# State space outputs of a fused two-block layer written feature by token instead of token by feature

## Chip, cores and metric

One core of a Trainium2 chip runs the whole program in one launch. The metric is the device time of that launch in microseconds (us), the median of three runs before the change.

## What is computed

Two transformer-like blocks on 512 tokens of width 1024, in fp32. The first has latent attention, chunked attention and a mixture of experts. The second has dilated attention and, beside it, a state space part with 16 heads of 64 features, 2 groups, state width 128 and chunks of 128 tokens; only this part and what surrounds it is touched. Cut to what matters:

```python
decay = jnp.exp(segsum(adt))                                   # per head, 128 x 128, lower triangle
cb = jnp.einsum('bclgn,bcsgn->bcgls', cc, bc)
y_diag = jnp.einsum('bcgjls,bcsgjp->bclgjp', cb[:, :, :, None] * decay, xg)   # inside a chunk
states = jnp.einsum('bcsgn,bcsgjp->bcgjpn', bc, xg * decay_to_end)
prev = ...                                                     # h = h * chunk_decay + state, chunk by chunk
y_off = jnp.einsum('bclgn,bcgjpn->bclgjp', cc, prev) * state_decay            # from the chunks before
y = y_diag + y_off + d_skip * xs_h                             # skip term
y_ssm = rms_norm_2(y * silu(z_ssm), ssm_norm_g)                # the gate z is a projection of the block's input
```

Then `y_att` and `y_ssm` go through one output projection (2048 to 1024), a residual and a layer norm.

## The kernel before, in words

Each engine has its own hand-written instruction list (`block.tensor`, `block.vector` for DVE, `block.scalar` for ACT, `block.gpsimd` for POOL, `block.sync` for SP's loads), tied together by counting semaphores. Within an engine, the order of the code is the order of execution. Activations lie feature by token (features on partitions, 512 tokens along the free axis) in eight tiles RA to RH of 128 x 8 x 512; the state space part works token by feature within a chunk.

**Gate tiles.** The 16 column tiles of the gate projection z (`gate_tile`, L1165, matmuls L689 to L691) are 24 matmuls of 128 x 512 each. Weights arrive in a ring of eight slots; ACT rounds each to fp32r (`hi`, L1411) and DVE takes the remainder (`lo`, L1788), so a gate tile needs both. Ten of the tiles are spread among the steps of the state space part, six follow. ACT evicts each with SiLU (`gate_out`, L1689); POOL multiplies it into the attention output RB (tiles 0 to 7) or the state space output (8 to 15) in `product` (L2661); ACT squares the product (`gated`, L1395) and DVE adds the squares (`sq_add`, L1793) for the norm. `stats_summed` (L745, L747) sums them over partitions; `root` (L1402, L1403) makes the factor.

**The state space part.** RG holds the convolved inputs feature by token, RH the same turned to token by feature (L1176). For each chunk c of four:

- PE spreads the cumulative sums over partitions (`spread_sums`, L1207, banks 2 and 3), DVE takes differences (L2382, 8 operations of 128 columns per half chunk), ACT the exponential (L1681), POOL the product with C times B (`decays`, L2643). The result is `decay`, a 128 x 128 matrix per head, in RE.
- POOL computes skip vector times x into RG (`skip_and_scale`, L2629), then scales x by dt in place in RH (L2633).
- PE multiplies, head by head, with `decay` stationary and the head's 64 columns of x moving: 16 matmuls into banks 4 and 5, token by feature (L1236). DVE adds the two banks onto RG (L2407).
- From chunk 1 on, PE multiplies C with the state (L1246, banks 0 and 1), DVE scales the result into `y_off` (L2415), scales the state (L2421) and adds `y_off` onto RG (L2422).
- POOL scales x for the states (`keys`, L2653), PE computes them into banks 4 and 5 (L1253), DVE sums them into the state (L2432, L2434).

PE's order for chunk c is: heads, first half of the next chunk's spreading, state output, gate tile 3 + 2c, states, second half of the spreading, gate tile 4 + 2c. After the fourth chunk and gate tile 9, PE turns the whole output back to feature by token: 32 turns of 128 x 128 in eight banks (L1264). DVE and ACT evict four banks each into RH (L1782, L1380). Then come the statistics of the attention half and gate tiles 10 to 15. The output projection (`parts`, L1271) takes each half as two fp32r parts: attention in RG and RE, state space in RF and RH.

Of the kernel before, what the change touches and what calls it, by code (L numbers as in the profile page):

```python
# [19 lines left out]
F32 = mybir.dt.float32  # L20
# [6 lines left out]
P = 128  # L27
# [49 lines left out]
def build(nc, xT_d, vec_d, rows_d, pos_d, rel_d, wr_d, wdt_d, pre_d, moe_d, post_d, out_d):  # L77
    ctx = ExitStack()
    with ctx:
# [139 lines left out]
        xg_tok, y_tokT = (r.rearrange("p (t h c) -> p t h c", t=TT, h=SSM_H) for r in (RHf, RGf))  # L219
# [135 lines left out]
        skip_ok = sem("skip_ok")  # L355
# [144 lines left out]
        PE_YT = PE_ZA + Z_BEHIND - 1  # L500
        PE_ZB = PE_YT + 8
        PE_OUT = PE_ZB + 16 - Z_BEHIND
        assert all(e % 2 == 0 for e in (PE_U, PE_OT, PE_O, PE_H, PE_Q2, PE_OT2, PE_XBC, PE_Z0, PE_YT, PE_ZB))

        def bank(e):
            if PE_XT <= e < PE_BT:
                return ps[e - PE_XT]
            if PE_YT <= e < PE_ZB:
                return ps[YT_BANKS[e - PE_YT]]
            return ps[(e - PE_Q2) % 4] if PE_Q2 <= e < PE_OT2 else ps[6 + e % 2]  # L510
# [24 lines left out]
        YT_BANKS = (0, 1, 4, 5, 6, 7, 0, 1)  # L535
# [119 lines left out]
        def _(pe):  # L655
# [3 lines left out]
            def free_bank(e):  # L659
# [8 lines left out]
                elif PE_YT <= e < PE_ZB:  # L668
                    pe.wait_ge(ev[e % 2], PE_YT // 2 + (e >= PE_YT + 6))
# [559 lines left out]
            for c in range(TT):  # L1229
                if c > 0:  # L1230
                    pe.wait_ge(state_ok, c)
                pe.wait_ge(xg_ok, c + 1)
                for h in range(SSM_H):
                    if h % 4 == 0:
                        pe.wait_ge(mm_ok, 4 * c + h // 4 + 1)
                    last = mm(ps[4 + h // 8][:, (h % 8) * 64:(h % 8) * 64 + 64], decay[:, h, :], xg_tok[:, c, h, :],  # L1236
                              start=True, stop=True)
                last.then_inc(yd_full, 1)

                if c < TT - 1:  # L1240
                    spread_sums(c + 1, (0, 1))
                if c > 0:
                    pe.wait_ge(cb_ok, 2)
                    pe.wait_ge(y_tok, c)
                    for g in range(2):
                        last = mm(ps[g][:, :], RF[:, 2 + g, c * P:(c + 1) * P], state[:, g, :], start=True, stop=True)  # L1246
                    last.then_inc(yo_full, 1)
                gate_tile(3 + 2 * c)
                if c < TT - 1:
                    pe.wait_ge(xgd_ok, c + 1)  # L1250
                    pe.wait_ge(yd_ok, c + 1)
                    for g in range(2):
                        last = mm(ps[4 + g][:, :], b_tok[:, g, c, :], REf[:, 2048 + g * T:2048 + (g + 1) * T], start=True, stop=True)  # L1253
                    last.then_inc(st_full, 1)
                    spread_sums(c + 1, (2, 3))
                    gate_tile(4 + 2 * c)

            pe.wait_ge(y_tok, TT)
            for i in range(8):
                e = PE_YT + i  # L1260
                t, hf = i // 2, i % 2
                free_bank(e)
                for c in range(4):
                    last = nc.tensor.transpose(bank(e)[:, c * P:(c + 1) * P],  # L1264
                                               RGf[:, t * D + (hf * 4 + c) * P:t * D + (hf * 4 + c + 1) * P], ident[:, :])
                last.then_inc(acc, 1)
# [4 lines left out]
            parts = (two(RGr, REr), two(RFr, RHr))  # L1271
# [94 lines left out]
        def _(act):  # L1366
# [324 lines left out]
            def gated(i):  # L1691
# [4 lines left out]
                else:  # L1696
                    k = i - KT
                    square(ST_SS, k, RH[:, k, :])
                    A(RFr[:, k, :], RH[:, k, :], ACT.Copy, scale=V("ssm_g", k)).then_inc(s_hi, 1)
# [28 lines left out]
            for i in range(1, 8, 2):  # L1728
                e = PE_YT + i
                evict(e, ([(RH[:, 4:8, (i // 2) * P:(i // 2 + 1) * P], quad(bank(e)[:, :]))], 1.0))  # L1730
# [7 lines left out]
            for i in range(Z_BEHIND, 16):  # L1738
# [5 lines left out]
                if i < Z_BEHIND + 4:  # L1744
                    j = 2 * (i - Z_BEHIND)
                    mix_parts(RGr, RB, (j, j + 1))
# [21 lines left out]
        def _(dve):  # L1768
# [631 lines left out]
            lo(M_Z + 4)  # L2400
            dve.wait_ge(sp2, 3)
# [363 lines left out]
```

## Time and profile before

| | |
|---|---|
| median of 3 runs | 1289.07 us (1288.01 to 1290.4) |
| the profiled execution, its own time | 1283.11 us |
| its span, first to last instruction | 1281.3 us |
| PE busy | 1201.3 us (94%) |
| DVE busy | 633.3 us (49%) |
| ACT busy | 464.3 us (36%) |
| POOL busy | 170.0 us (13%) |
| mean granted clock of TensorE | 0.979 |

Busy time is the union of an engine's instructions over the whole span; it says little about a stage of 75 us in it. The profiled execution is one run, and lies a little under the median of the three others. In the rows further down, PE is the matmul engine, PEld its weight loads; an fp32 matmul appears as two records (passes), and a record such as `128*64 128x128` names the part of the array used (rows * columns) and the moving operand.

### The profile page before, as it was taken

To read this page: it belongs to the slowest core of one execution; us is meant where nothing else is said; L and a number is where in the kernel's file an instruction comes from. 1 tells how busy PE (TensorE), PEld (TensorE's weight loads), DVE (VectorE), ACT (ScalarE), POOL (GpSimd) and SP (SyncE) were. 2 spreads that over 40 slices of the span, in tenths; PEclk is the share of its full clock that TensorE was granted. 3 is DMA by queue.
4 is the path that set the end of the run, shared out by engine and by line. 5 is a ranking of instruction groups with operands and counts; after the bars stand their busy time and mean duration, and the time that the engine had idled before them with its cause. 6 is when DMAs were issued, how large, how long until landed. Compare 5 with 4: busy or idle time off the path is not lost.

```text
span 1281.3 us, 17052 instructions
## 1 busy us (share of the span) xinstructions
PE 1201.3 (94%) x6666; PEld 863.8 (67%) x6666; DVE 633.3 (49%) x1167; ACT 464.3 (36%) x839; POOL 170.0 (13%) x145
## 2 busy tenths in 40 slices
PE   3899899999999999999999799999999999998995
PEld 0567676778887664455444378897558788777883
DVE  1755467654444454312101465334667666857546
ACT  3324346642222321111111351124665365655314
POOL 1300020000000000000000201600600038612003
PEclk8899999999999999999989899999999999999998
DMA  9565261023337559999999813321002221212301
GB/s 359 217 217 197 97 247 67 2 80 92 96 96 295 193 216 402 412 412 412 411 411 411 328 60 94 93 94 66 2 1 68 97 67 50 66 58 76 97 17 66
DMA packets 59166, 215.91 MB, mean 169 GB/s; under 512 B 4736, under 2 KB 5128, under 8 KB 59088
## 3 DMA queue, kind: packets, MB, share of 16 engines
q1 hardware_dynamic: 53040, 195.71, 41.8%
q10 hardware_dynamic: 3600, 10.21, 2.0%
q0 software_dynamic: 2448, 8.91, 1.9%
q8 instruction: 54, 0.88, 0.3%
q14 instruction: 24, 0.20, 0.0%
HBM read 200.37 MB, written 14.44 MB: 168 GB/s over the span
## 4 chain that ended last, share of the span: by engine, by line
PE 83%; DMA 5%; DVE 4%; issue 4%; ACT 4%; POOL 1%; SPq 0%; ACTq 0%; DVEq 0%; POOLq 0%
PE ps L689 13%; PE ps L691 12%; PE ps L690 12%; PE ps L993 7%; PE ps L975 5%; PE ps L1048 4%; PE ps L817 3%; PE ps L794 3%; PE ps L804 2%; DMA ring<-in_w_pre 2%; PE ps L730 2%; PE ps L732 2%; PE ps L731 2%; PE ps L759 2%; DMA ring<-in_w_moe 2%
## 5 line engine op out<-in xcount | busy, mean ns | idle before, releaser
L1788 DVE TENSOR_TENSOR ring_r<-ring,ring_r 128x1024 fp32r<-128x1024 f32 x115 | 143.6, 1251 | 185.4 <-ACT ring_r L1411 184.7
L1411 ACT ACTIVATE ring_r<-ring 128x1024 fp32r<-128x1024 f32 x116 | 121.4, 1053 | 206.1 <-PE ps L691 166.5
L689 PE MATMUL ps<-RB_r,ring_r 128*128 128x512 f32 x320 | 126.3, 395 | 1.1 <-DVE RH L1832 1.1
L691 PE MATMUL ps<-RB_r,ring_r 128*128 128x512 f32 x320 | 124.6, 389 | 0.0
L689 PE MATMUL ps<-RC_r,ring_r 128*128 128x512 f32 x224 | 90.1, 402 | 1.5 <-DVE ring_r L1788 1.2
L691 PE MATMUL ps<-RC_r,ring_r 128*128 128x512 f32 x224 | 87.3, 390 | 0.0
L690 PE MATMUL ps<-RD_r,ring_r 128*128 128x512 f32 x224 | 87.3, 390 | 0.0
L690 PE MATMUL ps<-RG_r,ring_r 128*128 128x512 f32 x208 | 81.0, 390 | 0.0
L689 PEld LDWEIGHTS ps<-RB_r,ring_r 128*128 128x128 f32 x320 | 60.1, 188 | 16.8 <-issue 4.5
L691 PEld LDWEIGHTS ps<-RB_r,ring_r 128*128 128x128 f32 x320 | 60.1, 188 | 12.6
L2608 POOL DMA_INDIRECT RC<-expert_rows,small x4 | 3.9, 963 | 457.7 <-DMA expert_rows<-RD 456.8
L2087 DVE TENSOR_SCALAR RH<-ps,small 128x256 f32<-128x256 f32 x64 | 28.0, 479 | 72.3 <-PE ps L975 72.1
L975 PE MATMUL ps<-RD_r,RC_r 128*128 128x256 f32 x256 | 61.3, 297 | 1.2 <-DVE RD_r L2067 1.2
L993 PE MATMUL ps<-ring,RH 128*64 128x512 f32 x272 | 61.3, 595 | 0.0
L2174 DVE TENSOR_TENSOR MASK<-RB,ps 128x256 f32<-128x256 f32 (+1 forms) x17 | 7.2, 421 | 105.3 <-ACT RB L1546 99.3
L975 PE MATMUL ps<-RD_r,RG_r 128*128 128x256 f32 x256 | 58.3, 283 | 0.0
L975 PEld LDWEIGHTS ps<-RD_r,RC_r 128*128 128x128 f32 x256 | 48.2, 200 | 12.6 <-issue 12.6
L1546 ACT ACTIVATE RB<-ps 128x256 f32<-128x256 f32 (+1 forms) x17 | 6.5, 384 | 133.2 <-PE ps L993 115.6
L730 PE MATMUL ps<-ring_r,RB_r 128*128 128x256 f32 x192 | 54.5, 284 | 0.2 <-DVE RF L1782 0.2
L732 PE MATMUL ps<-ring_r,RB_r 128*128 128x256 f32 x192 | 54.3, 283 | 0.0
L1424 ACT ACTIVATE SB<-ps,small 128x512 f32<-128x512 f32 (+1 forms) x64 | 40.2, 631 | 33.3 <-issue 17.3
L689 PEld LDWEIGHTS ps<-RC_r,ring_r 128*128 128x128 f32 x224 | 42.0, 188 | 13.4 <-issue 2.2
(496 smaller groups left out, 2652.2 us busy)
## 6 DMA issues: line engine op xcount, KB each, us to landing
ring<-in_w_moe SPq DMA_DIRECT2D x48, 1024.0 KB, 16.0
ring<-in_w_post SPq DMA_DIRECT2D x68, 512.0 KB, 3.6
ring<-in_w_pre SPq DMA_DIRECT2D x48, 512.0 KB, 3.7
ring<-in_w_pre SPq DMA_DIRECT2D x16, 1024.0 KB, 6.9
RE<-in_w_moe SPq DMA_DIRECT2D x16, 1024.0 KB, 14.1
RF<-in_w_moe SPq DMA_DIRECT2D x16, 1024.0 KB, 14.7
PQ<-in_w_moe SPq DMA_DIRECT2D x8, 1024.0 KB, 16.4
RB<-in_w_moe SPq DMA_DIRECT2D x8, 1024.0 KB, 16.7
```

Source lines behind the costliest of these rows:

```text
L689: mm(out, part(m)[:, w], xh(k), start=first and k == 0, stop=False)
L690: mm(out, part(m)[:, w], xl(k), start=False, stop=False)
L691: ins = mm(out, remainder(m)[:, w], xh(k), start=False, stop=last and k == n_k - 1)
L730: mm(out, xh(k)[:, tok], hi_w, start=(k == 0), stop=False)
L732: last = mm(out, xh(k)[:, tok], lo_w, start=False, stop=(k == KT - 1))
L794: mm(ps[2 * (n % 2) + s][:, 0:w], ql(2 * p + s, t), kr(2 * p + s, w), start=True, stop=True).then_inc(s_full, 1)
L975: last = mm(ps[GATHER_BANKS[i]][:, k % 2 * 256:k % 2 * 256 + 256], (h2_hi, h2_lo)[s][:, t, k * P:(k + 1) * P], OHr[:, quad % 2, t, :], sta ...
L993: last = mm(ps[2 + p % 2][u * SLOTS:(u + 1) * SLOTS, :], Xg[:, buf, kk, c:c + SLOTS], moe_tile(at + s, u, k), start=(kk == 0), stop=(kk == ...
L1048: last = mm(ps[4 + hf][u * SLOTS:(u + 1) * SLOTS, :], hidT[:, p % 2, f, u * SLOTS:(u + 1) * SLOTS], moe_tile(at + f, u, hf), start=(f == 0 ...
L1411: A(part(m), tile, ACT.Copy).then_inc(w_hi, 1)
L1424: A(probs(n)[:, s, 0:w], ps[2 * (n % 2) + s][:, 0:w], ACT.Exp, scale=-1.0, bias=nmax(n, s), accum_out=sums(n, s)).then_inc(p_ready, 1)
L1788: v.tensor_tensor(remainder(m), arrival(m)[2], part(m).bitcast(F32), ALU.subtract).then_inc(w_split, 1)
```

## The change

The output of the intra-chunk step is written feature by token at once.

- **Heads.** x (64 columns of a head) becomes the stationary operand and `decay` the moving one. The result is 64 features by 128 tokens; even heads go to partitions 0 to 63, odd ones to 64 to 127 of the same columns. Eight pairs fill banks 4 and 5.
- **State part.** For chunks 1 to 3, the scaled `y_off` is turned by PE (8 turns of 128 x 128) into banks 4 and 5 first, opening the accumulation to which the heads then add.
- **Skip term.** The product on POOL is gone. DVE evicts each 128 x 128 block with one operation, RG = RG * d + bank, with d as a column per feature (`d_col`, two small copies). RG keeps x feature by token until then and holds the output afterwards.
- **States** go to banks 0 and 1, directly behind the heads; POOL's `keys` moves ahead of the last two decay products. The differences for the first half of the next chunk now follow the state sum on DVE, and those of the second half open the next chunk.
- **Order on PE** for chunk c: state output, gate tile 2 + 2c, turns (these from chunk 1 on), heads, states, first half of the spreading, gate tile 3 + 2c, second half (these up to chunk 2). Then gate tile 9, statistics, gate tiles 10 to 15.
- The 32 final turns and their eight evictions are gone. RG and RH change places behind it (products, squares, the fp32r parts).

The diff, cut to its core:

```diff
@@ tensor @@
             for c in range(TT):
                 if c > 0:
                     pe.wait_ge(state_ok, c)
+                    for g in range(2):
+                        last = mm(ps[g][:, :], RF[:, 2 + g, c * P:(c + 1) * P], state[:, g, :], start=True, stop=True)
+                    last.then_inc(yo_full, 1)
+                    gate_tile(2 + 2 * c)
+                    pe.wait_ge(yd_ok, c)
+                    pe.wait_ge(y_tok, c)
+                    for k in range(KT):
+                        mm(ps[4 + k // 4][:, k % 4 * P:k % 4 * P + P], y_off[:, 2 * k:2 * k + 2, :], ident[:, :],
+                           start=(k % 4 == 0), stop=False, is_transpose=True)
                 pe.wait_ge(xg_ok, c + 1)
                 for h in range(SSM_H):
                     if h % 4 == 0:
                         pe.wait_ge(mm_ok, 4 * c + h // 4 + 1)
-                    last = mm(ps[4 + h // 8][:, (h % 8) * 64:(h % 8) * 64 + 64], decay[:, h, :], xg_tok[:, c, h, :],
-                              start=True, stop=True)
+                    out = ps[4 + h // 8][64 * (h % 2):64 * (h % 2) + 64, h // 2 % 4 * P:h // 2 % 4 * P + P]
+                    last = mm(out, xg_tok[:, c, h, :], decay[:, h, :], start=(c == 0), stop=(c == 0 or h % 8 >= 6))
                 last.then_inc(yd_full, 1)
 
                 if c < TT - 1:
+                    if c == 0:
+                        pe.wait_ge(cb_ok, 2)
+                    pe.wait_ge(xgd_ok, c + 1)
+                    for g in range(2):
+                        last = mm(ps[g][:, :], b_tok[:, g, c, :], REf[:, 2048 + g * T:2048 + (g + 1) * T], start=True, stop=True)
+                    last.then_inc(st_full, 1)
                     spread_sums(c + 1, (0, 1))
-                if c > 0:
-                    pe.wait_ge(cb_ok, 2)
-                    pe.wait_ge(y_tok, c)
-                    for g in range(2):
-                        last = mm(ps[g][:, :], RF[:, 2 + g, c * P:(c + 1) * P], state[:, g, :], start=True, stop=True)
-                    last.then_inc(yo_full, 1)
-                gate_tile(3 + 2 * c)
-                if c < TT - 1:
-                    pe.wait_ge(xgd_ok, c + 1)
-                    pe.wait_ge(yd_ok, c + 1)
-                    for g in range(2):
-                        last = mm(ps[4 + g][:, :], b_tok[:, g, c, :], REf[:, 2048 + g * T:2048 + (g + 1) * T], start=True, stop=True)
-                    last.then_inc(st_full, 1)
+                    gate_tile(3 + 2 * c)
                     spread_sums(c + 1, (2, 3))
-                    gate_tile(4 + 2 * c)
-
-            pe.wait_ge(y_tok, TT)
-            for i in range(8):
-                e = PE_YT + i
-                t, hf = i // 2, i % 2
-                free_bank(e)
-                for c in range(4):
-                    last = nc.tensor.transpose(bank(e)[:, c * P:(c + 1) * P],
-                                               RGf[:, t * D + (hf * 4 + c) * P:t * D + (hf * 4 + c + 1) * P], ident[:, :])
-                last.then_inc(acc, 1)
+
+            gate_tile(9)
             stats_summed(ST_AT, KT, 2)
@@ vector @@
+            for s in range(2):
+                ins = v.tensor_copy(d_col[64 * s:64 * s + 64, :], rows[64 * s:64 * s + 64, R_DSKIP + s:R_DSKIP + 16:2])
+            link(ins)
             dve.wait_ge(sp2, 3)
             for c in range(TT):
-                dve.wait_ge(skip_ok, c + 1)
-                dve.wait_ge(yd_full, c + 1)
-                for g in range(2):
-                    yt = y_tokT[:, c, 8 * g:8 * g + 8, :]
-                    ins = v.tensor_tensor(yt, yt, h8(ps[4 + g][:, :]), ALU.add)
-                link(ins)
-                dve.sem_inc(yd_ok, 1)
-                if c < TT - 1:
-                    differences(c + 1, (0, 1))
                 if c > 0:
+                    differences(c, (2, 3))
                     dve.wait_ge(yo_full, c)
...
-                    link(v.tensor_tensor(y_tokT[:, c, :, :], y_tokT[:, c, :, :], y_off, ALU.add))
-                dve.sem_inc(y_tok, 1)
-                sq_add_mixed(2 * c)
-                lo(M_Z + 5 + 2 * c)
+                    sq_add_mixed(2 * c - 1)
+                    lo(M_Z + 4 + 2 * c)
+                dve.wait_ge(yd_full, c + 1)
+                for k in range(KT):
+                    y = RG[:, k, c * P:(c + 1) * P]
+                    ins = v.scalar_tensor_tensor(y, y, d_col[:, k:k + 1], ps[4 + k // 4][:, k % 4 * P:k % 4 * P + P],
+                                                 ALU.mult, ALU.add)
+                ins.then_inc(yd_ok, 1)
                 if c < TT - 1:
-                    differences(c + 1, (2, 3))
                     dve.wait_ge(st_full, c + 1)
...
+                    differences(c + 1, (0, 1))
+                sq_add_mixed(2 * c)
+                lo(M_Z + 5 + 2 * c)
@@ gpsimd @@
                 decays(c, (0, 1))
                 product(2 * c)
-                if c == 0:
-                    keys(0)
+                if c < TT - 1:
+                    keys(c)
                 decays(c, (2, 3))
-                if 0 < c < TT - 1:
-                    keys(c)
                 product(2 * c + 1)
                 if c + 1 < TT:
-                    skip_and_scale(c + 1)
-            pool.wait_ge(ev[0], PE_ZB // 2)
-            pool.wait_ge(ev[1], PE_ZB // 2)
+                    scaled(c + 1)
+            pool.wait_ge(yd_ok, TT)
```

## Rows read from the trace of the kernel before

**Rows 1.** The page's chain that ended last, share of the span by engine.

```profile
PE 83%; DMA 5%; DVE 4%; issue 4%; ACT 4%; POOL 1%; SPq 0%; ACTq 0%; DVEq 0%; POOLq 0%
```

**Rows 2.** Windows, chunk 1: PE busy (x), PEld, DVE, ACT, POOL, PEclk, DMA.

```profile
1077.10:1097.60 20.50, 20.50 (x121) 16.03 (x120) 18.27 (x30) 12.02 (x14) 14.98 (x10) 1.00 0.18 52
```

**Rows 3.** Timeline of PE in chunk 1: start us, us, engine, line, tiles.

```profile
1077.14 3.68 PE L1236 MATMUL ps<-RH,RE 128*128 128x64 f32 x32
1080.74 1.16 PE L1207 MATMUL ps<-w_r,ident 64*128 64x128 f32 x16
1081.84 1.98 PE L1246 MATMUL ps<-RF 128*128 128x512 f32 x4
1083.26 0.79 PE L689 MATMUL ps<-RC_r,ring_r 128*128 128x512 f32 x1
...
1089.14 1.88 PE L1253 MATMUL ps<-RE,RF 128*128 128x512 f32 x4
1090.95 1.16 PE L1207 MATMUL ps<-w_r,ident 64*128 64x128 f32 x16
```

**Rows 4.** Timeline of PE, the last turns and the statistics.

```profile
1128.88 0.60 PE L1264 MATMUL ps<-ident,RG 128*128 128x128 f32 x4
1129.79 3.28 PE L1264 MATMUL ps<-ident,RG 128*128 128x128 f32 x28 [0.31 <-ACT SB L1689]
1132.90 1.02 PE L745 MATMUL ps<-PQ,ones 128*128 128x512 f32 x2
```

**Rows 5.** Timeline of PE in the attention, where two heads use the column halves.

```profile
901.71 0.66 PE L804 MATMUL ps<-ident,PQ 128*128 128x128 f32 x4
902.30 0.88 PE L817 MATMUL ps<-PTB,RE 128*64 128x128 f32 x12
903.11 0.49 PE L794 MATMUL ps<-RD,RC 64*128 64x128 f32 x4
...
907.35 1.09 PE L817 MATMUL ps<-PTB,RE 128*64 128x128 f32 x16
908.37 0.70 PE L794 MATMUL ps<-RD,RC 64*128 64x256 f32 x4
```

**Rows 6.** Timeline of DVE in chunk 1.

```profile
1080.93 1.29 DVE L2407 TENSOR_TENSOR RG<-RG,ps 128x512 f32<-128x512 f32 x2 [1.44 <-PE ps L1236]
...
1085.75 3.46 DVE L2421 TENSOR_TENSOR RF<-RF,MASK 128x512 f32<-128x512 f32 x2
1089.14 1.21 DVE L2422 TENSOR_TENSOR RG<-RG,RE 128x1024 f32<-128x1024 f32 x1
...
1092.24 2.15 DVE L2382 TENSOR_SCALAR RE<-ps,MASK 128x128 f32<-128x128 f32 x8
1094.31 1.28 DVE L2434 TENSOR_TENSOR RF<-RF,ps 128x512 f32<-128x512 f32 x2
```

**Rows 7.** Lines by form on DVE: count | busy us, mean ns.

```profile
L2460 DVE SCALAR_TENSOR_TENSOR RB<-RB,vec,RINV 128x512 f32<-128x512 f32 x8 | 8.7, 1130 | 0.0
...
L2247 DVE SCALAR_TENSOR_TENSOR RA<-ps,small,RA 128x512 f32<-128x512 f32 x8 | 6.0, 751 | 10.6 <-PE ps L1125 10.6
```

**Rows 8.** Timeline of POOL at the end of chunk 1.

```profile
1094.10 2.56 POOL L2643 TENSOR_TENSOR RE<-RE,OTK 128x512 f32<-128x512 f32 x2 [5.44 <-ACT RE L1681]
1096.61 2.90 POOL L2653 TENSOR_TENSOR RE<-RH,MASK 128x1024 f32<-128x1024 f32 x1
1099.47 1.72 POOL L2661 TENSOR_TENSOR RB<-RB,SB 128x512 f32<-128x512 f32 x1
```

**Rows 9.** Timeline of ACT after gate tiles 9 and 10.

```profile
1129.14 0.60 ACT L1689 ACTIVATE SB<-ps 128x512 f32<-128x512 f32 x1 [7.45 <-PE ps L691]
1129.63 0.62 ACT L1395 ACTIVATE PQ<-RB 128x512 f32<-128x512 f32 x1
...
1140.35 1.28 ACT L1689 ACT_TABLE_LOAD   x1 [1.75 <-PE ps L691]
```

**Rows 10.** Windows, as in rows 2, of the slice with the clock at half.

```profile
1172.00:1176.00 4.00, 4.00 (x12) 3.16 (x11) 3.55 (x5) 2.68 (x4) 0.60 (x2) 0.57 0.04 11
```

More of the change, by code:

```diff
@@ L217, in build @@
         chosen = OTK[:, 0, 0:TT * N_EXP].rearrange("p (t e) -> p t e", t=TT)
-        xg_tok, y_tokT = (r.rearrange("p (t h c) -> p t h c", t=TT, h=SSM_H) for r in (RHf, RGf))
+        xg_tok = RHf.rearrange("p (t h c) -> p t h c", t=TT, h=SSM_H)
+        d_col = small[:, 240:248]
         decay = REf[:, 0:2048].rearrange("p (h l) -> p h l", h=SSM_H)
@@ L499, in build @@
         PE_ZA = PE_BT + 2
-        PE_YT = PE_ZA + Z_BEHIND - 1
-        PE_ZB = PE_YT + 8
+        PE_ZB = PE_ZA + Z_BEHIND - 1
         PE_OUT = PE_ZB + 16 - Z_BEHIND
-        assert all(e % 2 == 0 for e in (PE_U, PE_OT, PE_O, PE_H, PE_Q2, PE_OT2, PE_XBC, PE_Z0, PE_YT, PE_ZB))
+        assert all(e % 2 == 0 for e in (PE_U, PE_OT, PE_O, PE_H, PE_Q2, PE_OT2, PE_XBC, PE_Z0, PE_ZB))
         def bank(e):
@@ L1269, in _ @@
                 gate_tile(i)
-            parts = (two(RGr, REr), two(RFr, RHr))
+            parts = (two(RHr, REr), two(RFr, RGr))
             for i in range(KT):
@@ L1697, in gated @@
                     k = i - KT
-                    square(ST_SS, k, RH[:, k, :])
-                    A(RFr[:, k, :], RH[:, k, :], ACT.Copy, scale=V("ssm_g", k)).then_inc(s_hi, 1)
+                    square(ST_SS, k, RG[:, k, :])
+                    A(RFr[:, k, :], RG[:, k, :], ACT.Copy, scale=V("ssm_g", k)).then_inc(s_hi, 1)
             hi(M_Z + 2)
@@ L1727, in _ @@
             gated(7)
-            for i in range(1, 8, 2):
-                e = PE_YT + i
-                evict(e, ([(RH[:, 4:8, (i // 2) * P:(i // 2 + 1) * P], quad(bank(e)[:, :]))], 1.0))
             root(5, ST_AT, KT, 2, eps2)
@@ L2431, in _ @@
                         if c == 0:
-                            ins = v.tensor_copy(sv, h8(ps[4 + g][:, :]))
+                            ins = v.tensor_copy(sv, h8(ps[g][:, :]))
                         else:
-                            ins = v.tensor_tensor(sv, sv, h8(ps[4 + g][:, :]), ALU.add)
-                    link(ins)
-                    dve.sem_inc(state_ok, 1)
-                    lo(M_Z + 6 + 2 * c)
-                    sq_add_mixed(2 * c + 1)
-            for i in range(8):
-                if i % 2 == 0:
-                    e = PE_YT + i
-                    evict(e, ([(RH[:, 0:4, (i // 2) * P:(i // 2 + 1) * P], quad(bank(e)[:, :]))], 1.0))
+                            ins = v.tensor_tensor(sv, sv, h8(ps[g][:, :]), ALU.add)
+                    ins.then_inc(state_ok, 1)
+                    dve.wait_ge(state_ok, c + 1)
+                    differences(c + 1, (0, 1))
+                sq_add_mixed(2 * c)
+                lo(M_Z + 5 + 2 * c)
             def state_rest(k):
                 dve.wait_ge(s_hi, k + 1)
-                v.scalar_tensor_tensor(RHr[:, k, :], RH[:, k, :], V("ssm_g", k), RFr[:, k, :].bitcast(F32), ALU.mult,
+                v.scalar_tensor_tensor(RGr[:, k, :], RG[:, k, :], V("ssm_g", k), RFr[:, k, :].bitcast(F32), ALU.mult,
                                        ALU.subtract).then_inc(s_lo, 1)
@@ L2658, in product @@
                 e = z_tile(i)
-                tile = RB[:, i, :] if i < KT else RH[:, i - KT, :]
+                tile = RB[:, i, :] if i < KT else RG[:, i - KT, :]
                 pool.wait_ge(ev[e % 2], e // 2 + 1)
```

21 lines of the change are left out of this document (6 added, 15 removed).

## The prediction

> **What bounds the kernel now.** I began with the chain that ended last: PE carries 83% of it [rows 1], so the question is what the change does to PE's own stream. The stage in question runs from 1058.4 us, where the first chunk's intra-chunk matmuls (L1236) begin, to about 1134 us. The window over chunk 1 shows PE busy for all of its 20.50 us, at full clock, with DVE at 18.27 and POOL at 14.98 [rows 2]. So in the loop no other engine stops PE, and a microsecond taken off PE's stream there is a microsecond, as long as the others keep up. DVE is close behind, which is where rivals come from. Durations are taken start to start, since a matmul's record overlaps the next one. An fp32 matmul is recorded as two passes.
>
> In chunk 1 the timeline of PE gives 3.60 us for the 16 heads of L1236 (32 passes), 1.10 for a spreading of sums, 7.30 for the state outputs (L1246) with the gate tile behind them, and 1.81 for the states (L1253); the second spreading and gate tile fill the window's last 6.65 us [rows 2, 3]. At the end the 32 turns of L1264 hold PE from 1128.88 to 1132.90, that is 4.02 us, 0.3 of it waiting for a bank [rows 4].
>
> **The intra-chunk matmuls.** They swap operands: x is stationary (64 columns), the decay matrix moves (128 columns), and even and odd heads write the two partition halves. The trace has this very form in the attention: L817, tile 128*64 with 128 moving columns, alternating halves. Twelve passes take 0.81 us to the next group, sixteen 1.02, so 0.0525 per pass and 0.18 fixed. Entering from the turns before costs 0.59 - 4 x 0.11 = 0.15 more [rows 5]. For 32 passes that is 1.68 + 0.33 = 2.01 us against 3.60, so 1.59 a chunk and **6.4 us** over four. Bounds: 1.7 (no switch cost) and 3.9 (no overlap of halves: 32 x 0.1125 + 0.33).
>
> The page TensorE: Matmul & The Clock Gate of the Trainium skill, section Part 3, says a weight load overlaps matmuls in flight only when their row groups differ; two column halves share their row groups, so by it loads and matmuls would alternate and this gain would shrink to about nothing. This case's trace disagrees: 0.0525 us a pass in rows 5 is under half the 0.1125 of L1236.
>
> **The turns.** The 32 final ones go: **4.02 us** off. Chunks 1 to 3 get eight each, of the state part alone, 24 in all. The last 28 of L1264 take 3.11 us, 0.111 each [rows 4], so **2.67 us** on. The form is the same, stationary data against the identity; that they open an accumulation is not priced. Bounds: 0.109 and 0.15 (four in 0.59 with their switch, rows 5).
>
> **What is moved.** States and state outputs keep their passes. The states use banks 0 and 1 and follow the intra-chunk matmuls at once, so POOL's product for them (L2653) is due one gate tile earlier, and it is placed before the last two decay products. PE's new waits are checked against durations. From the end of one chunk's heads to the start of the next PE works 1.81 + 6.65 + 1.10 + 7.30 + 0.89 = 17.75 us [rows 2 to 4]. Beside it runs a ring: the new evictions 2.15 on DVE, the state sum 1.28, the differences, exponentials and POOL's first pair 4.42 (1092.24 to 1096.66), POOL's gate product 1.72, its state product 2.90 and the last pair 2.56: 15.0 us [rows 6, 8]. The fourth group of heads is needed 1.4 us into the heads, so the room is **4.2 us**. State outputs, their scaling and the turns meet gate tiles of over 5 us in between. I cost all these waits at nothing; their cover is the gate tiles.
>
> **The evictions.** Per chunk DVE loses two sums of 512 (1.29) and in chunks 1 to 3 the sum over 1024 (1.21), and gets eight operations of 128 columns from PSUM with a scalar and an SBUF operand [rows 6]. The nearest is L2382, eight of 128 columns from PSUM in 2.15 us [rows 6]; the upper bound is the same kind at 512 columns, 0.75 each (L2247), 6.0 us [rows 7]. I take 2.15, by the row of equal width. DVE's chunk is then 18.27 - 2.50 + 2.15 = 17.9 us against PE's 20.50 - 1.59 + 0.89 = 19.8. The four turned evictions on DVE and four on ACT go as well, and POOL loses its skip product in each chunk. None of that is PE's time: nothing gained. The two small copies of the skip vector and SyncE's queue, which is unchanged, cost nothing.
>
> **A new wait at the end.** The statistics (L745, L747) now stand directly behind gate tile 9. The second needs the square of tile 7, which ACT makes after evicting gate tile 9: it ends at 1130.25, 1.37 after PE leaves the tile at 1128.88 [rows 4, 9]. The first statistic's two passes cover 0.90 of it (four passes of the same shape in L1253 take 1.81, rows 3), so **0.47 us** of stall appears where the turns gave cover. Bounds: nothing, and 1.3 if DVE's last evictions also delay the sum of squares.
>
> **Sum.** 6.4 + 4.02 - 2.67 - 0.47 = 7.3 us. What follows moves with it: ACT waits for PE's gate tile 10 (the table load at 1140.35, rows 9), and the exchange between ACT, DVE and POOL behind that is the same work under other tile names. The profiled execution took 1283.11 us and would take 1275.8. It stands 6.0 below the median of the runs, 1289.07, and I carry the same difference over: **1281.8 us**.
>
> **Rivals.**
> *The halves do not pair* (the change would not do what it says). At 0.1125 a pass the heads take 3.9 us, 0.3 more than before, four times: 7.3 - 6.4 - 1.3 is -0.4, so 1289.5 us. Rows 5 speak against it, as the form is the same; the decay operand is only in another tile. 4 in 100.
>
> *DVE becomes the bound.* If the eight evictions cost 0.75 each, DVE needs 18.27 - 2.50 + 6.0 = 21.8 us a chunk against 19.8: 2.0 us lost in three chunks, and about 1.3 at the end, which leaves nothing: 1289.1 us. The page TensorEngine Tiling (Array Packing) of the Trainium skill, section Performance Considerations, speaks for this one: tiling speeds up TensorE but not the emptying of PSUM, which should go over ScalarE and VectorE both, while this change leaves it on VectorE alone. Against it stands the 0.27 a piece of L2382. 4 in 100.
>
> *Evictions held by POOL, ending slower.* DVE operations with SBUF operands stretch beside POOL: L2460 takes 1.13 instead of 0.75 [rows 7], L2421 3.46 for two [rows 6]. The new evictions read and write SBUF. Eight at 1.13 are 9.0 us, 6.9 over my price: the ring exceeds its room by 2.7 in three chunks (8.1) and the last evictions with the sum of squares (0.7) overrun gate tile 9 (6.65 - 1.10, so 5.5) by 4.2. Together 12.3 lost, a net +5.0: 1294.1 us. It decides from about 1.05 each on. Against it: when the evictions are due, POOL has finished its last product and waits for exponentials of the next chunk. 4 in 100.
>
> *More than forecast.* Later, at 1172 us, a slice of 4 us has the clock at 0.57, so partly at the lower of its two levels; that costs 1.7 us [rows 10]. If the shifted work meets it otherwise, it may vanish: 1289.1 - 7.3 - 1.7 = 1280.1 us. It may also come longer, which the main case's range holds. 5 in 100.
>
> **How the numbers follow.** A measurement of this kernel can tell about 0.2%, 2.6 us. The forecast has 83 in 100, the clock case 5, the three others 4 each. Faster: 83 + 5 = 0.88; same: the first two rivals, 0.08; slower: 0.04. The main case's own range, with the bounds partly used up (a switch cost twice as high, turns at 0.15, 1.3 of stall, the clock either way), is 1279 to 1286. It holds 8 in 10 or more with the clock case, so the range stays there.
>
> **What would show it.** L1236's successor as tile 128*64 with 32 passes in about 2.0 us start to start; three groups of eight turns at 0.9 us; no idle of PE between 1058 us and the end of gate tile 9, 6.4 - 2.7 = 3.7 us earlier than now, and gate tile 10 about 7.3 earlier; the eight evictions in about 2.2 us; then an idle of half a microsecond before L747. The forecast is wrong if PE waits for POOL's products within the heads, if the evictions take over 5 us, or if the halves' passes start more than 0.06 us apart.

## The result and the profile after

The changed kernel takes 1277.24 us (median of eight runs, 1276.13 to 1281.51) against 1288.08 for the kernel before (eight runs, 1281.95 to 1290.40). The two medians lie 10.8 us apart. The ratio worked out over all these executions is 0.9934, with a 95% interval of 0.9915 to 0.9953: 8.5 us faster, between 6 and 11. The forecast was 7.3 us, a ratio of 0.9943. The changed kernel was measured again with the experiments: 1277.58 against 1286.09 us, ratio 0.994 (0.9917 to 0.9963).

Line numbers have moved: L1236 is now L1240, L1207 is L1201, L1246 is L1227, L1253 is L1248, L1264 has become L1233, L689 to L691 are L683 to L685, L745 and L747 are L739 and L741, L1788 is L1773, L1395 is L1383, L1793 is L1778, L2382 is L2367, L2643 is L2620, L2653 is L2630. The page of the changed kernel, busy time and the chain that ended last:

```profile
PE 1198.7 (94%) x6658; PEld 856.4 (67%) x6658; DVE 631.7 (49%) x1186; ACT 461.5 (36%) x835; POOL 166.4 (13%) x141
...
PE 82%; DMA 5%; DVE 4%; ACT 4%; issue 4%; POOL 1%; SPq 0%; ACTq 0%; DVEq 0%; POOLq 0%
```

PE still carries the chain, as in [rows 1]. The timeline of PE in chunk 1 (start us, us, engine, line, tiles), which answers to [rows 3]:

```profile
1075.40 1.99 PE L1227 MATMUL ps<-RF 128*128 128x512 f32 x4
1076.82 0.79 PE L683 MATMUL ps<-RC_r,ring_r 128*128 128x512 f32 x1
...
1082.71 1.03 PE L1233 MATMUL ps<-ident,RE 128*128 128x128 f32 x8
1083.68 1.97 PE L1240 MATMUL ps<-RE,RH 128*64 128x128 f32 x32
1085.58 1.98 PE L1248 MATMUL ps<-RE,RF 128*128 128x512 f32 x4
1087.49 1.16 PE L1201 MATMUL ps<-w_r,ident 64*128 64x128 f32 x16
...
1094.25 1.16 PE L1201 MATMUL ps<-w_r,ident 64*128 64x128 f32 x16
```

From one line's start to the next: state output and gate tile 7.31 us (1075.40 to 1082.71), the eight turns 0.97, the heads 1.90, the states 1.91, a spreading 1.09. No row has an idle time. The end of the stage, which answers to [rows 4]:

```profile
1131.05 1.02 PE L739 MATMUL ps<-PQ,ones 128*128 128x512 f32 x2
1132.48 1.12 PE L741 MATMUL ps<-PQ,ones 128*128 128x512 f32 x2 [0.41 <-ACT PQ L1383]
1133.04 0.79 PE L683 MATMUL ps<-RC_r,ring_r 128*128 128x512 f32 x1
```

The 32 turns are gone, and before the second statistic there is an idle time of 0.41 us that ends with ACT's square (L1383). The two statistics take 1.99 us to the next gate tile; the kernel before took 1.32 (1132.90 to 1134.22).

Windows of the changed kernel over chunks 0, 1 and 2, each from its heads to the next (us, then busy time of PE, PEld, DVE, ACT, POOL, then PEclk, DMA share, GB/s), which answer to [rows 2]:

```profile
1063.70:1083.65 19.95, 19.95 (x129) 14.89 (x128) 17.38 (x35) 11.20 (x14) 16.45 (x11) 1.00 0.18 54
1083.65:1103.60 19.95, 19.95 (x129) 14.89 (x128) 19.48 (x35) 11.70 (x15) 12.89 (x8) 1.00 0.19 53
1103.60:1123.55 19.95, 19.95 (x129) 14.89 (x128) 14.89 (x33) 11.70 (x15) 13.32 (x8) 1.00 0.17 53
```

PE is busy throughout, at full clock. DVE is at 19.48 of 19.95 us in the second window (chunk 1), more than the 17.9 that the prediction had for it; this becomes important below.

**Where the time went.** I compare stretches between the same instructions of two traces: from the first turn of x (before the state space part) to the end of the span, and from the first head to the first matmul of gate tile 10 ("the stage").

| | before | changed | difference |
|---|---|---|---|
| span | 1281.3 | 1279.5 | -1.8 |
| start of the first turn of x | 1037.80 | 1043.06 | +5.3 |
| first turn of x to the end | 243.50 | 236.44 | **-7.06** |
| of it ahead of the first head | 20.59 | 20.68 | +0.1 |
| of it the stage | 75.83 | 69.30 | -6.53 |
| gate tile 10 to the end | 147.08 | 146.46 | -0.6 |

The span is read to a tenth, so the stretches to the end are good to 0.05 us. Nearly all of the gain lies in the stage, where it was forecast. The profiled execution of the changed kernel hides most of it, because it arrived 5.3 us later at a part that the change does not touch. The next section shows where that comes from.

### The profile page after: what moved, and what is told of

Its sections match the earlier page's. It is cut to its first block, busy times and chain, and to the rows that moved or that the text cites. A ratio compares the mean times of both kernels' runs of the same rounds, so it can differ in the third digit from the quotient of the medians.

```text
span 1279.5 us, 17035 instructions
## 1 busy us (share of the span) xinstructions
PE 1198.7 (94%) x6658; PEld 856.4 (67%) x6658; DVE 631.7 (49%) x1186; ACT 461.5 (36%) x835; POOL 166.4 (13%) x141
## 4 chain that ended last, share of the span: by engine, by line
PE 82%; DMA 5%; DVE 4%; ACT 4%; issue 4%; POOL 1%; SPq 0%; ACTq 0%; DVEq 0%; POOLq 0%
PE ps L683 13%; PE ps L685 12%; PE ps L684 12%; PE ps L987 8%; PE ps L969 4%; PE ps L1042 4%; PE ps L811 3%; PE ps L788 3%; PE ps L798 2%; DMA ring<-in_w_pre 2%; PE ps L724 2%; PE ps L726 2%; PE ps L725 2%; PE ps L753 2%; DMA ring<-in_w_moe 2%
## 5 line engine op out<-in xcount | busy, mean ns | idle before, releaser
L1773 DVE TENSOR_TENSOR ring_r<-ring,ring_r 128x1024 fp32r<-128x1024 f32 x115 | 146.9, 1280 | 187.9 <-ACT ring_r L1399 187.1
L683 PE MATMUL ps<-RB_r,ring_r 128*128 128x512 f32 x320 | 126.3, 395 | 1.1 <-DVE RH L1817 1.1
L685 PE MATMUL ps<-RB_r,ring_r 128*128 128x512 f32 x320 | 124.6, 389 | 0.0
L684 PE MATMUL ps<-RG_r,ring_r 128*128 128x512 f32 x272 | 106.0, 390 | 0.0
L683 PE MATMUL ps<-RC_r,ring_r 128*128 128x512 f32 x224 | 90.1, 402 | 1.3 <-DVE ring_r L1773 1.0
L685 PE MATMUL ps<-RC_r,ring_r 128*128 128x512 f32 x224 | 87.3, 390 | 0.0
L683 PEld LDWEIGHTS ps<-RB_r,ring_r 128*128 128x128 f32 x320 | 60.1, 188 | 16.8 <-issue 4.5
L685 PEld LDWEIGHTS ps<-RB_r,ring_r 128*128 128x128 f32 x320 | 60.1, 188 | 12.7
L684 PEld LDWEIGHTS ps<-RG_r,ring_r 128*128 128x128 f32 x272 | 51.1, 188 | 11.3 <-issue 1.0
```

The costliest lines, as they stand in the source:

```text
L683: mm(out, part(m)[:, w], xh(k), start=first and k == 0, stop=False)
L684: mm(out, part(m)[:, w], xl(k), start=False, stop=False)
L685: ins = mm(out, remainder(m)[:, w], xh(k), start=False, stop=last and k == n_k - 1)
L1773: v.tensor_tensor(remainder(m), arrival(m)[2], part(m).bitcast(F32), ALU.subtract).then_inc(w_split, 1)
```

## The experiments

All are edits of the changed kernel. The stage is the measure, since it does not contain the varying part. Where one execution was made, the table says so. The kernel before, taken beside them, was at 1286.00 us for the unpaired heads, no turns and DVE 8 and 24, at 1286.09 for the changed kernel again, the cover, the statistics inside and POOL, and at 1284.03 (one run) for the full weights and DVE 4.

| run | stage, us | turn of x to end, us | time, us |
|---|---|---|---|
| before | 75.83 | 243.50 | 1288.08 |
| changed | 69.30 | 236.44 | 1277.24 |
| changed, again | 69.30 | 236.48 | 1277.58 |
| unpaired heads | 71.74 | 238.95 | 1279.76 |
| full weights | 75.26 | 240.96 | 1287.02 (one run) |
| no turns | 66.64 | 232.46 | 1273.69 |
| 28 turns as cover | 71.69 | 238.80 | 1282.51 (one run) |
| statistics inside | not comparable | 235.76 | 1278.19 |
| POOL 3 x 1.9 us more | 69.29 | 236.44 | 1279.34 |
| DVE 4 operations more | 69.81 | 236.93 | 1276.58 (one run) |
| DVE 8 more | 74.57 | 240.42 | 1284.86 |
| DVE 24 more | 93.09 | 260.32 | 1300.45 (one run) |

**The changed kernel again.** No edit.

> The changed kernel once more, as a partner for the others, and to see how much of the time between runs arises before the changed stage. Theory: from the first turn of x (L1170) to the end it is 236.4 us in every run, against 243.5 in the kernel before, while the time ahead of it varies by up to 5 us with the clock granted in the expert stage between 640 and 690 us. Rival (the change also shifts the stages ahead of it): the time ahead of L1170 is different from that of the kernel before in every run.

The stretch from the turn of x is 236.48 us; the turn itself starts at 1038.42 instead of 1043.06. Two traces of one kernel differ by 4.6 us ahead of the change. The window from 640 to 690 us, in the expert stage, shows it (last columns: granted clock, DMA share, GB/s). The kernel before:

```profile
640.00:690.00 50.00, 46.83 (x225) 23.67 (x224) 6.07 (x12) 5.29 (x12) 0.00 (x0) 0.93 1.03 411
```

The changed kernel:

```profile
640.00:690.00 50.00, 46.83 (x202) 24.73 (x202) 5.65 (x11) 4.29 (x9) 0.00 (x0) 0.83 1.00 390
```

The changed kernel again:

```profile
640.00:690.00 50.00, 46.83 (x225) 23.68 (x223) 6.07 (x12) 5.27 (x11) 0.00 (x0) 0.93 1.03 411
```

PE is busy equally long in each, but at a granted clock of 0.93, 0.83 and 0.93. At 0.83 instead of 0.93, 5 us of 50 are lost. Matched matmul by matmul, the two traces of the changed kernel are within 0.2 us of each other at 648 us and 4.9 us apart at 673, so nearly all of the distance arises in this window. Over all twelve traces, the four with 0.93 reach the turn of x between 1037.57 and 1038.42 us, the one with 0.90 at 1038.08, and the seven with 0.86 or less between 1040.46 and 1044.04. The rival, that the change itself shifts the earlier stages, falls: the changed kernel is in both groups. Why the clock falls deeper in some executions stays open. It accounts for a spread of 5 us between single executions. That it is also why the medians differ by 10.8 where the traces differ by 7.1 is likely but not shown, since the other executions left no trace.

**Unpaired heads.** Within a bank, the four even heads come first in the program, then the four odd ones.

```diff
-                for h in range(SSM_H):
-                    if h % 4 == 0:
-                        pe.wait_ge(mm_ok, 4 * c + h // 4 + 1)
+                for n in range(SSM_H):
+                    h = n // 8 * 8 + n % 4 * 2 + n // 4 % 2
+                    if n % 8 == 0:
+                        pe.wait_ge(mm_ok, 4 * c + n // 4 + 2)
```

> The changed kernel with the heads of a bank in another order: the four even ones, then the four odd ones, so that consecutive matmuls lie in the same half of PE's columns; the work is the same. Measure: start to start from the heads (L1240) to what follows, 1.90 us in the changed kernel, and the stage from the first head to the first matmul of gate tile 10, 69.30 us there. Theory (the gain on the heads comes from neighbours in different halves running side by side): passes go from 0.054 to about 0.107 us, heads from 1.90 to 3.5 us, the stage 4 x 1.6 = 6.4 us longer, the whole kernel 6 us slower than the changed one. Rival (the 64-column weight load is what is cheaper, and the order does not matter): heads stay near 1.9 us and the stage at 69.3.

Timeline of PE, heads and states of chunk 1:

```profile
1084.06 2.57 PE L1241 MATMUL ps<-RE,RH 128*64 128x128 f32 x32
1086.56 1.98 PE L1249 MATMUL ps<-RE,RF 128*128 128x512 f32 x4
```

The heads (chunk 1 in the timeline of PE) take 2.50 us to the states instead of 1.90, so +0.6 and not +1.6; the stage grows by 2.44. Ratio to the kernel before: 0.9954 (0.9934 to 0.9974). By the total, the order matters but is the smaller part, and that led to the next run. The single passes say otherwise. Timeline of PE over the first 0.47 us of the heads of chunk 1, with the number of passes begun, in the changed kernel and in this run:

```profile
1083.68 0.66 PE L1240 MATMUL ps<-RE,RH 128*64 128x128 f32 x8
```

```profile
1084.06 0.65 PE L1241 MATMUL ps<-RE,RH 128*64 128x128 f32 x4
```

In the changed kernel the passes begin in pairs, 0.006 us apart, one in each half, and after the first 0.160 each half begins its next pass 0.109 us later. In this run the passes of one group (four heads, eight passes, one half) begin 0.109 us apart as well. But the next group, in the other half, does not wait for the end of it: it begins 0.493 us after the group ahead, when five of that group's eight passes have begun. The third group can be told by its wait for the second bank's products: its first pass begins when 13 passes have begun, while 16 stand ahead of it in the program. So PE drew it forward, and apart from the first and the last half microsecond the halves still ran side by side. Three times 0.493 us and the whole of a last group make the 2.50 us. The run therefore removed only part of the pairing; the 0.073 us a pass that the next expectation takes from it is no price of one half. Where nothing runs beside them, in the first five and the last five passes, the starts lie 0.109 apart (0.160 behind the very first).

**Full weights.** The stationary operand is the x of two heads, 128 columns, and all 128 partitions are written.

```diff
-                    out = ps[4 + h // 8][64 * (h % 2):64 * (h % 2) + 64, h // 2 % 4 * P:h // 2 % 4 * P + P]
-                    last = mm(out, xg_tok[:, c, h, :], decay[:, h, :], start=(c == 0), stop=(c == 0 or h % 8 >= 6))
+                    out = ps[4 + h // 8][:, h // 2 % 4 * P:h // 2 % 4 * P + P]
+                    last = mm(out, xg_tok[:, c, h // 2 * 2:h // 2 * 2 + 2, :], decay[:, h, :], start=(c == 0), stop=(c == 0 or h % 8 == 7))
```

> Each of the 64 head matmuls takes two heads' x (128 columns) as stationary operand and writes all 128 partitions; every output block gets a wrong sum, with the same number of matmuls and the same moving operand. With neighbours in one half (the run before) a pass cost 0.073 us, in alternate halves 0.054, and in the kernel before (128 weight columns, 64 moving) 0.112. Theory (most of the gain on the heads is that 64 instead of 128 weight columns are loaded per pass; the alternation is the smaller part): heads at 0.105 to 0.112 a pass, 3.4 to 3.6 us, the stage 6 us longer than 69.30. Rival (the gain is the swap of operands, long moving against short): heads stay under 2.6 us.

Timeline of PE, the same place:

```profile
1086.04 3.74 PE L1240 MATMUL ps<-RE,RH 128*128 128x128 f32 x32
1089.62 1.88 PE L1248 MATMUL ps<-RE,RF 128*128 128x512 f32 x4
```

3.58 us for the same 32 passes of 128 moving columns, practically the 3.60 of [rows 3] with 64 moving columns. So the swap of operands by itself gives nothing. The forecast time came, but not the reason for it. In the first 0.47 us five passes begin:

```profile
1086.04 0.72 PE L1240 MATMUL ps<-RE,RH 128*128 128x128 f32 x5
```

They lie 0.112 us apart, and those of one half with 64 weight columns 0.109. The narrower weights by themselves therefore give next to nothing either: 32 passes all in one half would take 3.6 us by my estimate from 0.109, although no run has that order for a whole chunk. What takes the heads from 3.6 to 1.90 us is that two halves run side by side; the narrower weights are the condition for it. The page TensorE: Matmul & The Clock Gate of the Trainium skill, section Part 2, says that a weight load takes time in proportion to its columns. The records of the loads are 0.192 us with 128 columns and 0.137 with 64, longer but not twice as long, and the passes hardly move apart for it. By the rule in Part 3 of that page of the Trainium skill, cited in the prediction, the two halves would hold each other up; pairs that begin 0.006 us apart contradict that.

**No turns.** The heads open their banks themselves.

```diff
-                    for k in range(KT):
-                        mm(ps[4 + k // 4][:, k % 4 * P:k % 4 * P + P], y_off[:, 2 * k:2 * k + 2, :], ident[:, :],
-                           start=(k % 4 == 0), stop=False, is_transpose=True)
...
-                    last = mm(out, xg_tok[:, c, h, :], decay[:, h, :], start=(c == 0), stop=(c == 0 or h % 8 >= 6))
+                    last = mm(out, xg_tok[:, c, h, :], decay[:, h, :], start=True, stop=True)
```

> Leaves out the 24 turns of the state part, so the contribution of earlier chunks to the output is missing. Theory: each group of eight costs PE what it takes start to start (0.97 us), so the stage falls from 69.30 to 66.4 us and the kernel by 2.9. Rival (the turns stand in time in which PE would wait for the decay products anyway): the stage stays within 0.5 us of 69.3 and a wait appears before the heads.

Timeline of PE, heads and states of chunk 1; the row ahead of them is now a matmul of the gate tile:

```profile
1082.68 1.97 PE L1237 MATMUL ps<-RE,RH 128*64 128x128 f32 x32
1084.58 1.98 PE L1245 MATMUL ps<-RE,RF 128*128 128x512 f32 x4
```

The stage falls by 2.66 us, 0.89 for each group, with the heads starting straight behind the gate tile. The heads' own 1.90 are unchanged. The turns are time on PE, as priced (2.67); ratio to the kernel before 0.9913 (0.9879 to 0.9948). The stretch behind gate tile 10 was 1.3 us shorter as well: there PE's clock stayed at 1.00 between 1140 and 1200 us, where the changed kernel has 0.97, the counterpart of [rows 10].

**28 turns as cover.** Turns of the identity into banks 0 and 1, read by nobody, between gate tile 9 and the statistics.

```diff
             gate_tile(9)
+            for k in range(28):
+                nc.tensor.transpose(ps[k // 4 % 2][:, k % 4 * P:k % 4 * P + P], ident[:, :], ident[:, :])
             stats_summed(ST_AT, KT, 2)
```

> 28 turns of the identity into two free banks between gate tile 9 and the statistics, whose results nobody reads. Theory (the removed final turns were pure time on PE apart from the cover that they gave): they cost 28 x 0.11 = 3.1 us, less the wait of 0.67 us before the second statistic that they now cover, so the stage grows from 69.30 to 71.7 us. Rival (the final turns were hidden by what ACT does at that point): under 1 us longer.

Timeline of PE at the end of the stage:

```profile
1129.80 3.22 PE L1256 MATMUL ps<-ident 128*128 128x128 f32 x28
1132.85 1.02 PE L739 MATMUL ps<-PQ,ones 128*128 128x512 f32 x2
1133.71 1.02 PE L741 MATMUL ps<-PQ,ones 128*128 128x512 f32 x2
```

The turns take 3.05 us to the first statistic, the idle time before the second is gone, and the stage is 2.39 us longer: 3.05 less 0.66. The final turns that the change removed were PE's time, less the wait that they covered.

**Statistics inside.** The second statistic goes behind the sixth matmul of gate tile 10.

```diff
-            stats_summed(ST_AT, KT, 2)
-            for i in range(Z_BEHIND, 16):
+            pe.wait_ge(sq_used, ST_AT + KT - 2)
+            mm(ps[2][:, :], ones[:, :], SQ[:, 1, :], start=True, stop=False).then_inc(sq_used, 1)
...
+                if k == 1:
+                    pe.wait_ge(sq_ready, ST_AT + KT)
+                    mm(ps[2][:, :], ones[:, :], SQ[:, 0, :], start=False, stop=True).then_inc(sq_used, 1)
```

> The second matmul of the statistics moves from ahead of gate tile 10 to behind the sixth matmul of it. Theory (PE waits 0.41 us and exposes a weight load there because the turns that covered ACT's square are gone): the wait goes, gate tile 10 ends about 0.7 us earlier and the kernel is 0.7 us faster than the changed one. Rival (the root that ACT makes from the statistics is what sets the later exchange, so later statistics cost as much as the wait): no difference or up to 0.5 us slower.

Timeline of PE, the two statistics with the matmuls of gate tile 10 around the second:

```profile
1128.73 1.02 PE L1256 MATMUL ps<-PQ,ones 128*128 128x512 f32 x2
1129.18 0.80 PE L1262 MATMUL ps<-RC_r,ring_r 128*128 128x512 f32 x1
...
1130.98 1.02 PE L1267 MATMUL ps<-PQ,ones 128*128 128x512 f32 x2
1131.44 0.80 PE L1262 MATMUL ps<-RC_r,ring_r 128*128 128x512 f32 x1
```

No idle time is left, and the turn of x to the end takes 235.76 us, 0.7 less than the changed kernel. The theory holds in the trace. The median, 1278.19 us (ratio to the kernel before 0.9936, 0.9915 to 0.9957), cannot tell it from the changed kernel; 0.7 us is below what these runs resolve.

**POOL's load.** The skip product is given back to POOL for chunks 1 to 3, into an unused tile.

```diff
                 if c + 1 < TT:
+                    g.tensor_tensor(PTB[:, :, :].rearrange("p a (h c) -> p (a h) c", h=8), xg_tok[:, c + 1, :, :],
+                                    rows[:, R_DSKIP:R_DSKIP + 16].unsqueeze(2).to_broadcast([P, SSM_H, SSM_P]), ALU.mult)
                     scaled(c + 1)
```

> Gives POOL the skip product back before each scaling of chunks 1 to 3, written to an unused tile: 1.9 us more on POOL in each of three chunks. Theory (POOL's relief was worth nothing): the stage stays within 0.3 us of 69.30. Rival (POOL's load or its stretching of DVE's operations was part of what bounds the stage): 1 to 5 us longer.

The stage is 69.29 us. Taking the product from POOL was worth nothing, as forecast; ratio 0.995 (0.9931 to 0.9969).

**DVE's load.** Further operations of 128 columns from PSUM into an unused tile, ahead of the eight evictions: 8, 24 and 4 of them (with 24, DVE also waits for its own results after each eight).

```diff
                 dve.wait_ge(yd_full, c + 1)
+                for x in range(8):
...
+                    ins = v.tensor_scalar(PTB[:, x // 4 % 2, x % 4 * P:x % 4 * P + P], ps[4 + x // 4 % 2][:, x % 4 * P:x % 4 * P + P],
+                                    d_col[:, 0:1], None, ALU.mult)
                 for k in range(KT):
```

> Eight more operations of 128 columns from PSUM (into an unused tile) ahead of the eight evictions of each chunk: 2.15 us more on DVE per chunk, inside the ring from the heads over DVE, ACT and POOL to the next heads. Theory (PE bounds the stage, the ring has room; in the changed kernel's trace POOL's last product of chunks 2 and 3 ends about 2.2 us before the heads need it): the stage stays within 0.5 us of 69.30. Rival (DVE is or is nearly the bound, since it has more work per chunk than any engine but PE): the stage grows by up to 3 x 2.15 = 6.5 us.

With eight more, the timeline of PE at the second spreadings of chunks 1 and 2:

```profile
1090.44 1.16 PE L1201 MATMUL ps<-w_r,ident 64*128 64x128 f32 x16 [1.10 <-DVE RE L2367]
...
1112.79 1.16 PE L1201 MATMUL ps<-w_r,ident 64*128 64x128 f32 x16 [2.34 <-DVE RE L2367]
1113.88 3.56 PE L1227 MATMUL ps<-RF 128*128 128x512 f32 x4
```

And the windows over chunks 1 and 2 (columns as above):

```profile
1078.70:1099.80 21.10, 20.00 (x129) 14.89 (x128) 21.02 (x42) 11.81 (x15) 12.72 (x8) 1.00 0.15 50
1099.80:1123.80 24.00, 21.66 (x129) 15.48 (x128) 22.89 (x43) 11.75 (x15) 14.49 (x9) 0.93 0.14 44
```

My theory fell. The stage is 5.3 us longer, which eats most of the gain (ratio to the kernel before 0.9987, 0.9968 to 1.0007). PE waits, but not for POOL's products: it waits in front of the second spreading (L1201) until DVE's differences (L2367) have freed the banks, 1.10 us in chunk 1 and 2.34 in chunk 2. The windows show DVE busy for 21.02 of 21.10 us, then 22.89 of 24.00. The second wait also cost clock: 0.93 in that window, and the state output behind it took 2.57 us to the gate tile instead of 1.42. Of the 4.1 us that this chunk grew, 2.3 are the wait, and the rest lies in matmuls at the lower level.

> The same with 24 more operations, about 6.9 us more on DVE per chunk. Theory with the room of 4.2 us that the prediction worked out: 2.7 us lost in each of three chunks and 4.3 at the end, the stage 12 us longer. With the room of about 2.5 us that the changed kernel's trace suggests: 4.4 in each of three and 4.3 at the end, 17 us longer. Rival (DVE already binds): 3 x 6.9 + 6 = 27 us longer.

With 24 more, two of the waits in the timeline of PE:

```profile
1099.29 2.08 PE L1201 MATMUL ps<-w_r,ident 64*128 64x128 f32 x16 [4.60 <-DVE RE L2367]
...
1149.15 2.07 PE L739 MATMUL ps<-PQ,ones 128*128 128x512 f32 x2 [3.63 <-DVE PQ L1778]
```

23.8 us longer, more than either room would give and less than 27. The waits of PE add up to 16.3 (3.55, 4.60 and 4.53 ahead of spreadings, 3.63 for the sum of squares); the rest is matmuls at the lower clock, behind these waits.

> Four more operations of 128 columns on DVE ahead of the evictions of each chunk, about 1.1 us, half of the run with eight, which made the stage 5.3 us longer. DVE is busy for 19.48 of 19.95 us in chunk 2 of the changed kernel. Theory (DVE is within half a microsecond of binding there): the stage grows by 0.3 to 1.5 us. Rival (a ring of dependences has 2 us of room, and the loss with eight came from the clock that fell): within 0.2 us of 69.30.

With four more, the only wait in the loop:

```profile
1109.23 1.16 PE L1201 MATMUL ps<-w_r,ident 64*128 64x128 f32 x16 [0.46 <-DVE RE L2367]
```

0.51 us longer, all of it in one wait in chunk 2. So at 1.1 us more per chunk DVE just binds; at 2.15 it costs 1.1 us in chunk 1 and 4.1 in chunk 2.

## Why the prediction was right, and where it was not

**The heads.** Forecast 3.60 to 2.01 us, measured 1.90; the states behind them take 1.91 instead of 1.81 and the turns ahead of them 0.97 instead of 0.89, so the switches cost what was allowed for, in other rows. Reading the price off L817 [rows 5] was right, since it has the same form in all respects: 0.0545 us a pass, half of the 0.109 at which either half goes on. The reason given holds too: the 1.7 us a chunk come from the halves that run side by side. The rival "the halves do not pair" put the heads at 3.9 us; from 0.109 a pass they would take 3.6 (an estimate), so the change would have gained nothing on them, near what the rival said.

**The turns.** 4.02 us removed: the stage with 28 of them put back confirms their rate, 0.109 each. 2.67 added: measured 2.66 by taking them out.

**The wait at the end.** Forecast 0.47 us, measured 0.67: 0.41 of idle time and the start of the second statistic behind it, whose weight load then lies open. The step was right, its size 0.2 too small.

**The spreadings.** Not in the sum: behind a gate tile a spreading starts 0.09 us later than it did behind the states, in three chunks. The stage then adds up from the prediction's terms (7.24 before rounding): the heads give 0.36 more than forecast, the states cost 0.31, the turns 0.24 and the wait 0.20 more, the spreadings 0.27, which leaves 6.6; 6.53 was measured.

**What follows.** Forecast to move along unchanged: it is 0.6 us shorter, which with the 0.1 ahead of the first head brings the whole to 7.06. The clock falls once in this stretch in both traces, so that is not the reason. Half of it is one wait of PE for a remainder, 1.25 us before and 0.96 now; 0.3 lies behind the last matmul. The changed kernel's second trace has both again. Why they are shorter stays open.

**The evictions.** Forecast 2.15 us for eight by L2382, measured 2.16. With the first eight of a chunk, from the timeline of DVE in chunk 0, come the two copies of the skip vector:

```profile
1063.32 2.48 DVE L2387 COPY small<-rows 64x8 f32<-64x8 f32 x2
1065.86 2.16 DVE L2408 SCALAR_TENSOR_TENSOR RG<-RG,small,ps 128x128 f32<-128x128 f32 x8
```

The two copies were to cost nothing. They take 2.48 us, but they end at 1065.8, when the heads have just finished.

**The room.** This step failed, though the time did not show it: the prediction gave the new waits 4.2 us of room by one ring and DVE 17.9 of 19.8 us a chunk. In chunk 1 DVE had 0.5 left. Lines by form on DVE, 1058 to 1135 us, kernel before and changed:

```profile
L1788 DVE TENSOR_TENSOR ring_r<-ring,ring_r 128x1024 fp32r<-128x1024 f32 x8 | 11.9, 1482 | 4.7 <-ACT ring_r L1411 4.7
```

```profile
L1773 DVE TENSOR_TENSOR ring_r<-ring,ring_r 128x1024 fp32r<-128x1024 f32 x8 | 15.3, 1908 | 4.3 <-ACT ring_r L1399 4.1
...
L2408 DVE SCALAR_TENSOR_TENSOR RG<-RG,small,ps 128x128 f32<-128x128 f32 x32 | 8.6, 342 | 5.7 <-PE ps L1240 5.7
```

The remainders for the gate weights (L1788, now L1773) went from 1.48 to 1.91 us each. In [rows 6, 7] such stretching beside POOL is visible, and I had put it on the new evictions (they were not touched: 342 ns each) instead of on what DVE already had. POOL's last pair of products in chunk 2 stretched too, 2.56 to 4.04 us:

```profile
1096.18 1.90 POOL L2630 TENSOR_TENSOR RE<-RH,MASK 128x1024 f32<-128x1024 f32 x1
1098.83 4.04 POOL L2620 TENSOR_TENSOR RE<-RE,OTK 128x512 f32<-128x512 f32 x2 [0.75 <-ACT RE L1669]
```

And with more work on DVE, the wait that came first was one that I had not listed: the second spreading, which needs the differences of the first half. In chunk 1 the change is 0.5 us away from the second rival. The page TensorEngine Tiling (Array Packing) of the Trainium skill, section Performance Considerations, cited for that rival, says that the emptying of PSUM may come to bind. Here it is DVE's work as a whole, of which the evictions are 2.15 us a chunk: the runs with 4 and 8 more operations show the boundary at about 1 us of DVE work. It did not decide here because eight evictions of 0.27 us replace sums of about the same cost.

**The range.** 1279.0 to 1286.0 was given; the median of 1277.24 lies 1.8 us under it. Measured by the ratio, 0.9934 of the 1289.07 us that the forecast started from is 1280.6, inside it and 1.2 us under the 1281.8. The carrying over from one profiled execution to the median is the step behind the difference. It took the profiled execution as a fixed distance from the median, while either can lie on any side of the fall of the clock in the expert stage. How often the unprofiled runs of each kernel met it isn't known. From the turn of x to the end, the forecast was off by 0.2 us, and that is partly luck: the stage gave 0.7 us less than the sum, and 0.6 came from behind it, where nothing had been forecast.

## What to carry to other kernels

If one operand of a small fp32 matmul has only 64 columns, as in the heads here, make it the stationary one and write alternate halves: here the swap without halves gained nothing (3.58 us for 3.60), and two halves side by side took 1.90. An order of the program that is meant to prevent the pairing need not do so: read such a test by when single passes start, and not by its total alone. Before an edit that shortens PE's stream, add up the busy time of the next engine per iteration with its stretched durations, and list every bank that PE reuses: here the wait that appeared stood at the first reused bank, not at the ring that had been added up. When single executions spread by more than the effect, compare the stretch between two fixed instructions, not the whole time.

## What the runs showed of the hardware

- fp32 passes begin 0.112 us apart with 128 weight columns, whether 64 or 128 columns move. With 64 weight columns and 128 moving they begin 0.109 apart in one half, and those of the other half run beside them, 0.006 later: 32 passes take 1.90 us instead of 3.58.
- With the halves in groups of eight passes, PE began the next group when five passes of the group ahead had begun, before three that stand earlier in the program: 2.50 us for 32 passes.
- In the stage, waits of PE of 2.34, 3.55, 4.60, 4.53 and 3.63 us went with matmuls at the lower clock level behind them; waits of 0.41, 0.46 and 1.10 us did not.
- The remainder on DVE (128x1024, two SBUF operands) took 1.22 us in the three cases of the kernel before in which POOL was idle, and 1.40 to 1.70 beside POOL; in the changed kernel it took up to 2.92. An eviction (128x128, one operand in PSUM) took 0.34 with POOL at work and without.
- A copy of 64 x 8 elements on DVE took 1.24 us beside POOL, where eight operations of 128 x 128 from PSUM took 2.16.
- In the expert stage the granted clock over 640 to 690 us was between 0.83 and 0.93 for the same part of the program, worth up to 5 us of the whole.
